# Fillers in the on-chip memory layout of a bidirectional encoder layer, so that the mixer's and the MLP's buffers start at the same offset within 512 bytes as the weights' slots

## What is computed

```
hn   = modulated_rms_norm(h, sh1, sc1)
proj = hn @ w_in                       # 2048 x 5664
attn = axial_gqa_attention(...)        # 8 query heads, 2 kv heads, 128 wide
dn   = bidir_gated_deltanet(...)       # 8 heads, both directions, with a 3-tap convolution before it
h    = h + gt1 * (concat(attn, dn) @ w_out)
hn   = modulated_rms_norm(h, sh2, sc2)
u    = dwconv_centred(hn @ w_up, w_ffn_conv) + b_ffn_conv      # w_up: 2048 x 11264
h    = h + gt2 * ((silu(u_gate) * u_val) @ w_down)             # w_down: 5632 x 2048
out  = rms_norm(h) * final_norm
```

## The kernel before, in words

| buffers | before | after |
| --- | --- | --- |
| `act_hi`, `act_lo`, `raw`, `w_hi`, `w_lo`, `cst_sb` | 128 | 128 |
| `wba_hi`, `wba_lo`, `xs` | 352 | 128 |
| mixer: `ktok`, `vtok`, `va`, `mixed`, `ada_w`, `ada_acc`, `lvl` | 352 | 128 |
| mixer: `pre` | 96 | 128 |
| mixer: `ka`, `act3`, `tmp`, `DD`, `EG`, `CL`, `T`, `PTb`, `XT`, `Wc`, `Zc`, `qr`, `vs` | 128 | 128 |
| MLP: `mh_hi`, `mh_lo`, `rstd`, `gp` | 352 | 128 |
| MLP: `cv`, `prod`, `hn2`, `hT`, `sqacc`, `sq` | 384 | 128 |

## Time and profile before

### The profile page before, as it was taken

The page is one execution under the profiler, slowest core; times in us unless marked ns, Lnnn a source line. Parts: engine busy times, 40 slices in busy tenths (PEclk is TensorE's granted clock), DMA queues, the critical chain, the costliest instruction groups (busy, mean ns, idle before and its releaser), DMA issues.

```text
span 2705.2 us, 35982 instructions
## 1 busy us (share of the span) xinstructions
PE 2603.7 (96%) x12454; PEld 2130.1 (79%) x12454; DVE 1408.0 (52%) x1830; ACT 1029.2 (38%) x1438; POOL 214.4 (8%) x286
## 2 busy tenths in 40 slices
PE   4899999999999989989999999999999999999997
PEld 4777887888888868866888888887888888888885
DVE  3644666666666666455444444444344443444454
ACT  5224354354354344334443234442244432232334
POOL 2320211211211212000000000000000000000000
PEclk9888999999999989999999999999999999999998
DMA  8752544544544535432332333333333333333333
GB/s 289 273 171 61 156 124 125 155 122 127 155 119 129 152 87 155 128 85 73 98 101 82 95 102 93 101 92 91 103 94 93 98 88 93 103 98 93 88 91 125
DMA packets 431810, 318.47 MB, mean 118 GB/s; under 512 B 12902, under 2 KB 403857, under 8 KB 431249
## 3 DMA queue, kind: packets, MB, share of 16 engines
q1 hardware_dynamic: 401648, 212.19, 27.3%
q0 software_dynamic: 29184, 104.87, 12.2%
q10 hardware_dynamic: 929, 0.74, 0.1%
HBM read 313.56 MB, written 4.19 MB: 117 GB/s over the span
## 4 chain that ended last, share of the span: by engine, by line
PE 92%; DVE 3%; DMA 2%; ACT 1%; issue 1%; DVEq 0%; ACTq 0%; POOL 0%; POOLq 0%
PE pw L1355 23%; PE pw L1357 22%; PE pw L1356 22%; PE pw L1339 2%; PE pw L1341 2%; PE pw L1340 2%; PE pd L1622 2%; PE pd L1645 1%; PE pd L1658 1%; PE pd L1605 1%; DMA EG<-in_w_ada_dram 1%; PE pd L1665 1%; PE pd L1419 1%; DMA va<-in_w_ada_dram 1%; PE pd L1449 1%
## 5 line engine op out<-in xcount | busy, mean ns | idle before, releaser
L1355 PE MATMUL pw<-act_hi,w_hi 128*128 128x512 f32 x2016 | 814.9, 404 | 14.9 <-DVE act_lo L1250 8.8
L907 DVE TENSOR_TENSOR w_lo<-raw,w_hi 128x1024 fp32r<-128x1024 f32 x426 | 520.8, 1223 | 544.2 <-ACT w_hi L547 541.7
L1357 PE MATMUL pw<-act_hi,w_lo 128*128 128x512 f32 x2016 | 789.1, 391 | 0.0
L1356 PE MATMUL pw<-act_lo,w_hi 128*128 128x512 f32 x2016 | 787.3, 391 | 0.0
L547 ACT ACTIVATE w_hi<-raw 128x1024 fp32r<-128x1024 f32 x426 | 450.2, 1057 | 543.2 <-PE pw L1357 427.0
L1355 PEld LDWEIGHTS pw<-act_hi,w_hi 128*128 128x128 f32 x2016 | 380.5, 189 | 108.2 <-issue 24.7
L1357 PEld LDWEIGHTS pw<-act_hi,w_lo 128*128 128x128 f32 x2016 | 380.0, 188 | 82.2
L1356 PEld LDWEIGHTS pw<-act_lo,w_hi 128*128 128x128 f32 x2016 | 380.8, 189 | 80.1 <-issue 6.9
L1355 PE MATMUL pw<-mh_hi,w_hi 128*128 128x512 f32 x704 | 280.4, 398 | 1.1 <-DVE w_lo L907 1.1
L1356 PE MATMUL pw<-mh_lo,w_hi 128*128 128x512 f32 x704 | 278.3, 395 | 0.0
L1357 PE MATMUL pw<-mh_hi,w_lo 128*128 128x512 f32 x704 | 278.3, 395 | 0.0
(11 more groups left out here) (280 smaller groups left out, 2684.3 us busy)
## 6 DMA issues: line engine op xcount, KB each, us to landing
raw<-in_w_up_dram SPq DMA_DIRECT2D x176, 512.0 KB, 3.9
ada_w<-in_w_ada_dram POOLq DMA_DIRECT2D x128, 512.0 KB, 4.4
raw<-in_w_in_dram SPq DMA_DIRECT2D x84, 512.0 KB, 3.9
raw<-in_w_down_dram SPq DMA_DIRECT2D x64, 384.0 KB, 3.4
raw<-in_w_down_dram SPq DMA_DIRECT2D x64, 320.0 KB, 3.1
raw<-in_w_out_dram SPq DMA_DIRECT2D x32, 512.0 KB, 4.4
DD<-in_w_ada_dram POOLq DMA_DIRECT2D x8, 512.0 KB, 8.4
mixed<-in_x_dram SPq DMA_DIRECT2D x4, 1024.0 KB, 13.8
```

Of the source, the lines that this page charges most:

```text
L907: V.tensor_tensor(w_lo[slot][:], raw[slot][:], w_hi[slot][:].bitcast(F32), ALU.subtract).then_inc(lo_made.sem, 1)
L1355: M(bank, w_hi[slot][:, k, :], hi[:, k0 + k, :], start=first, stop=False)
L1356: M(bank, w_hi[slot][:, k, :], lo[:, k0 + k, :], start=False, stop=False)
L1357: ins = M(bank, w_lo[slot][:, k, :], hi[:, k0 + k, :], start=False, stop=last)
```

## The change

It allocates four buffers that nothing reads or writes. No instruction is added, removed or moved; only addresses change.

```diff
@@ -139,6 +139,7 @@
         nrm = sb("nrm", [P, 3, NB])
+        sb("to_row", [P, 72])
@@ -153,7 +154,9 @@
         lvl = sb("lvl", [P, LEVELS, P], BF16, mixer)
+        sb("after_lvl", [P, 64], F32, mixer)
         pre = sb("pre", [P, 3, S + 2], F32, mixer)
+        sb("after_pre", [P, 120], F32, mixer)
         ka = sb("ka", [P, KV_HEADS, S], F32, mixer)
@@ -207,6 +210,7 @@
         gp = sb("gp", [P, 2, S + 2], F32, mlp)
+        sb("after_gp", [P, 120], F32, mlp)
         cv = sb("cv", [P, 2, S], F32, mlp)
```

## The result

The median fell from 2704.25 us to 2691.72 us (5 runs, 2690.28 to 2692.02), a ratio of 0.9949 with a 95% interval of 0.9939 to 0.996. That is 12.5 us; five runs of the kernel before lie between 2702.0 and 2708.01 us. The profiled execution of the changed kernel took 2691.72 us with a span of 2689.9 us. In the kernels of the experiments they lie elsewhere again by a line or a few, and the operands' names tell which matmul is meant.

What follows compares the result with a forecast made beforehand. TensorE, busy 96% of the span, was taken as the bound; 11.0 + 2.6 - 0.5 = 13.1 us off 2704.25 gave 2691.1 us, with a range of 2686 to 2701.

Steps and rivals of the forecast that it cites:

- The signs named ahead: Down-projection window of 120 us holds 531 matmuls, heads last as long as before, `mh` matmuls' mean lengths fall about 7 ns.
- One sign of being wrong: The prediction would be wrong if more than 2 us came from the first 1200 us.
- (a): Down-projection tiles without transposes ahead: 50 tiles x 33 matmuls x 6.67 ns, 11.0 us gained.
- The wait for `w_lo`: Second unit of each chunk's first down tile: wait grows by 0.1 us, giving back 0.5 us in all.
- (b): The last chunk's 14 down-projection tiles after transposes: first 11 distances gain 0.04 us, other 22 gain 0.147; 2.6 us.
- That the address is not the cause: Rival: the down-projection stays at 233.3 ns for a reason of its own; 2704.3 us, chance 0.12.
- That only part of the offset counts: Rival: with period 1024, some down-projection triples keep their cost; about half, 6.5 us, 2697.7 us, chance 0.06.
- That a common phase makes the engines collide: Rival: same-phase VectorE or ScalarE accesses slow 4224 up-projection matmuls, costing 28.2 us; 2719.3 us, chance 0.08.
- The rule of lines of 16 bytes: Skill rule on SBUF: 352 and 128 are both multiples of 16, so columns cost the same and the sum is 0.
- I take the address: Operand addresses, not unit length or engine company, make down-projection matmuls 233.3 ns against the up-projection's 226.7.
- On the weights' side I took 0: Weights `wba_hi`, `wba_lo` of 48 matmuls, moved 352 to 128: gain 0, bounds 0 and 0.3 us.

Runs made afterwards that it cites:

- experiment 2: Changed kernel with the MLP's buffers back at 352 and 384, the mixer's still at 128; 2705.5 us over 10 runs, ratio 1.0.
- experiments 1: Kernel before with one filler of 288 bytes ahead of `mh_hi`, the mixer as before; 2691.77 us, ratio 0.9951.
- experiment 3: Changed kernel with 224 bytes ahead of everything, so all operands at 352 and distances kept; 2694.5 us, one run.
- experiment 4: Changed kernel with the slots `raw`, `w_hi` and `w_lo` moved by 32 bytes to 160, all else at 128; 2741.78 us, one run.
- experiment 10: Changed kernel with `w_lo` alone 32 bytes further than `act`, `mh` and `w_hi`; 2741.3 us, one run.

## Why the prediction was right

**What it rested on held.** TensorE's stream was the bound, VectorE and ScalarE had nothing to give (752, 692 and 632 ns of the earlier trace rows stand within 1 ns in the changed kernel), and the difference of 6.67 ns between the earlier trace rows vanished altogether. Predicted were 2691.1 us and 13.1 us less; the median is 2691.72 us, 12.5 us less. The signs named ahead came too: 532 matmuls in the window for 531, the heads as long as before (720.98 and 720.96 us), and the mean lengths of the matmuls with `mh` down by 6 ns for 7 (from 398, 395 and 395 to 392, 389 and 389). One sign of being wrong came as well: more than 2 us from the first 1200 us, the 2.98 us between the two profiled executions. It takes experiment 2 to show that they are not the change's.

**The terms.** (a) A chunk without transposes was to give 16 x 33 x 6.67 ns = 3.52 us less the 0.12 us of the first unit, 3.40 us; it gave 3.26. The wait for `w_lo` grew as foreseen, from the 0.23 us of the earlier trace rows to 0.36; in the changed kernel, timeline of PE:

```profile
1463.97 0.39 PE L1361 MATMUL pw<-mh_hi,w_lo 128*128 128x512 f32 x1
1464.71 0.50 PE L1359 MATMUL pw<-mh_hi,w_hi 128*128 128x512 f32 x1 [0.36 <-DVE w_lo L911]
```

From 0.63 us between the two starts it went to 0.74. The remaining 0.14 us of a chunk lie in its first two tiles: behind such a wait, and again at the start of the second tile, the changed kernel's matmuls run unevenly, as after transposes (the ten distances from the second matmul of the waiting unit on are 224 to 240 ns), and I had applied the full 6.67 ns to them. The other 14 tiles gain all of it. (b) The tiles after transposes: the first 11 distances of such a tile, after the change,

```profile
2595.47 0.48 PE L1359 MATMUL pw<-mh_hi,w_hi 128*128 128x512 f32 x1
...
2598.09 0.39 PE L1361 MATMUL pw<-mh_hi,w_lo 128*128 128x512 f32 x1
```

take 2.62 us, where an output tile had promised 2.61 and the tile before took 2.65. The last chunk, counted as 14 such tiles and 2 plain ones, was put at 2.6 + 0.44 - 0.12 = 2.9 us and gave 2.5. The trace has transposes ahead of 13 of its tiles, not 14, which changes the sum by only 0.03 us. Both terms were some 5 to 15% too large, and the sum 12.3 against 13.1 us.

**The rivals.** That the address is not the cause is refuted by experiments 1 and 2: moving the MLP's buffers alone makes and unmakes the gain. That only part of the offset counts, with a period of 1024 bytes, is refuted by the changed kernel itself, all of whose down matmuls run at 226.7 ns though `mh` stands 640 and `act` 128 beyond a multiple of 1024. The grain is finer than the prediction's 512 bytes and not coarser: d = 256 is as good as 0. That a common phase makes the engines collide is refuted by the up-projection's unchanged 972 matmuls. The rule of lines of 16 bytes from "SBUF — State Buffer" of the Trainium skill, in its specifications, can't explain what was measured: starts at multiples of 16 differ by 6.7 ns a matmul as the distance to the weights goes from 224 to 0, and by 10 ns between d = 256 and d = 240 behind transposes. Whether it has a part in the 238 ns of d = 4 no run here separates; its starts are no multiples of 16, but neither are those of d = 8, which run at 232 to 233.3 ns.

**Where the reading was too coarse.** "I take the address" left open whether the moving operand's own offset or its distance to the weights counts; I wrote both into one sentence. Both give the same forecast for this change, and so it was safe, but they are different rules: by the first, experiment 3 would have cost 55 us, and by the second experiment 4 nearly that. On the weights' side I took 0 from the gate columns, at a distance of 288 from `act`. That bound was no good guide: experiment 10 shows that an offset of the weights alone costs the full 6.7 ns in loads of 128 columns. For the gate columns themselves 0 was right: in the changed kernel, at distance 0, ten of their distances take 2.30 us (120.36 to 122.66), no less than the 2.29 of the earlier trace rows. They load 32 columns and stand in a short stretch; which of the two makes them insensitive no run here separates.

## What to carry to other kernels

Where TensorE streams 512 columns of 4-byte data behind a new 128 x 128 weight load each time, at full clock, compare the pace of otherwise equal matmuls in different stages before anything else: start-to-start distances from the timeline, or counts in windows. If they differ by whole cycles without a wait, look at the distance between the start of what streams and the start of the weights, and make it 0, or 256 bytes, which cost the same here, for every buffer of the stream; fillers cost nothing but room, and a stray 32 bytes ahead of the weights' slots cost this kernel 50 us. The mixer's alignment in this change was worth nothing; one filler ahead of `mh_hi` does it all.

## What the runs showed of the hardware that was not expected

- The pace of these matmuls at 2.4 GHz depends on the distance between moving operand and weights, not on either's own offset: 226.7 ns with all at 128 and with all at 352, 233.3 ns with the slots 32 bytes on. At the 1.2 GHz level it does not: 427 ns at d = 480.
- Distances of 0 and 256 bytes are equal, 64 and 320 are (228.7 and 228.8 ns), 128 and 384 nearly; 64 bytes the other way (192, 448) cost the full 6.7 ns. The dearest that was tried was 4 bytes, 238 ns.
- At some distances the pace also depends on how the stream began: d = 128 ran at 232.5 ns in chunks 0 and 2 and at 233.3 in chunks 1 and 3, d = 240 at 233.3 ns in tiles without transposes ahead and at 237 behind them. What decides between them no run here shows.
- It doesn't add up by matmul: one weight load of three, or one moving operand of three, 32 bytes out of phase brings the mean pace of the three to 233 ns, and two moving operands of three to 231.1.
- What happens between the two reads inside TensorE or SBUF no run here shows. That both streams draw on something shared whose turn depends on the address is an argument from the period, not a measurement.
